# Query, key and value projections in 256-column items, with the attention heads run between their row tiles, in a hybrid decoder step on one core

## What is computed

```
hn = _rmsnorm(x, norm_w)
u = hn @ w_in
z_ssd, xbc, dt_raw, q, k, v, z_att, g_ssd, g_att = jnp.split(u, _split_points(), axis=-1)
...
q = _rope(_rmsnorm(q.reshape(b, t, ATT_HEADS, ATT_HEAD_DIM), q_norm_w), pos)
k = _rope(_rmsnorm(k.reshape(b, t, ATT_HEADS, ATT_HEAD_DIM), k_norm_w), pos)
...
for g, (win, dil) in enumerate(ATT_GROUPS):
    ...
alpha = jax.nn.softmax(jnp.stack(lses, axis=-1), axis=-1)
```

## Time and profile before

| | |
|---|---|
| median of 3 runs | 1186.77 us (1186.63 to 1190.5) |
| profiled execution, its own time | 1187.57 us |
| its span (first to last instruction) | 1185.8 us |
| mean granted TensorE clock | 0.94 of full speed |
| PE busy | 1097.8 us (93%) |
| weight loads busy | 1010.2 us (85%) |
| DVE, ACT, POOL busy | 656.7, 499.4, 219.8 us (55%, 42%, 19%) |
| first row-tile matmul | 18.95 us |
| column stream behind the last head | 426.50 us |

### The profile page before, as it was taken

How to read it: one execution, slowest core, us unless ns; L and a number is a source line. 1 busy time by engine, 2 the same in 40 slices (tenths; PEclk the granted TensorE clock), 3 DMA queues, 4 the chain that set the end, 5 groups by cost and what they waited for, 6 DMA issues and landing times.

```text
span 1185.8 us, 19650 instructions
## 1 busy us (share of the span) xinstructions
PE 1097.8 (93%) x7838; PEld 1010.2 (85%) x7838; DVE 656.7 (55%) x936; ACT 499.4 (42%) x1130; POOL 219.8 (19%) x209
## 2 busy tenths in 40 slices
PE   4999989999999989895999999999998999689998
PEld 3887779977988779775999899898998999689998
DVE  6663527622462347237677677776764466834342
ACT  5334533345333544102554645656445566612210
POOL 0330003400231000000211220221120589500000
PEclk9998899989999899756999999999999999789999
DMA  8546102580242047145056246254446899432221
GB/s 348 213 169 276 55 1 116 213 329 1 107 168 81 1 151 246 58 152 232 1 219 235 109 162 254 110 218 163 182 175 273 343 360 343 155 144 80 100 98 46
DMA packets 29819, 198.14 MB, mean 167 GB/s; under 512 B 4104, under 2 KB 6280, under 8 KB 20224
## 3 DMA queue, kind: packets, MB, share of 16 engines
q1 hardware_dynamic: 25712, 183.35, 40.5%
q0 software_dynamic: 4016, 13.54, 3.0%
HBM read 180.16 MB, written 104.70 MB: 240 GB/s over the span
## 4 chain that ended last, share of the span: by engine, by line
PE 73%; DVE 11%; ACT 7%; issue 4%; DMA 2%; POOL 2%; SPq 0%; DVEq 0%; ACTq 0%; POOLq 0%
PE bank L618 36%; PE bank L590 16%; DVE cacc L1575 2%; PE bank L813 2%; PE bank L715 2%; ACT wH L1136 2%; PE bank L678 2%; PE bank L767 2%; POOL t L1080 2%; PE bank L884 1%; PE bank L654 1%; DVE wL L1511 1%; DMA slot<-in_state_ssm 1%; PE bank L902 1%; PE bank L876 1%
## 5 line engine op out<-in xcount | busy, mean ns | idle before, releaser
L1511 DVE TENSOR_TENSOR wL<-w_raw,wH 128x2048 fp32r<-128x2048 f32 (+1 forms) x63 | 145.0, 2302 | 155.0 <-ACT wH L1136 152.9
L618 PE MATMUL bank<-xH,wH 128*128 128x260 f32 x976 | 207.9, 294 | 8.1 <-DVEq L1455 6.9
L618 PE MATMUL bank<-xH,wL 128*128 128x260 f32 x976 | 198.1, 285 | 0.0
L618 PE MATMUL bank<-xL,wH 128*128 128x260 f32 x976 | 197.8, 284 | 0.0
L1136 ACT CAST wH<-w_raw 128x2048 fp32r<-128x2048 f32 (+1 forms) x63 | 119.2, 1892 | 136.2 <-PE bank L618 84.8
L618 PEld LDWEIGHTS bank<-xH,wH 128*128 128x128 f32 x976 | 152.0, 191 | 18.8 <-issue 16.6
L618 PEld LDWEIGHTS bank<-xH,wL 128*128 128x128 f32 x976 | 152.0, 190 | 0.0
L618 PEld LDWEIGHTS bank<-xL,wH 128*128 128x128 f32 x976 | 152.0, 190 | 0.0
L590 PE MATMUL bank<-wH,xH 128*128 128x512 f32 x336 | 136.7, 407 | 10.0 <-DVE xL L1490 6.0
L590 PE MATMUL bank<-wH,xL 128*128 128x512 f32 x336 | 134.6, 401 | 0.0
L590 PE MATMUL bank<-wL,xH 128*128 128x512 f32 x336 | 134.6, 401 | 0.0
(11 more groups left out here) (285 smaller groups left out, 1916.9 us busy)
## 6 DMA issues: line engine op xcount, KB each, us to landing
w_raw<-in_weights SPq DMA_DIRECT2D x62, 1024.0 KB, 5.3
out_kvs<-in_cache SPq DMA_DIRECT2D x16, 2044.0 KB, 10.2
ring<-in_cache SPq DMA_DIRECT2D x48, 256.0 KB, 3.2
slot<-in_state_ssm SPq DMA_DIRECT2D x16, 512.0 KB, 5.9
out_ssm_s<-slot POOLq DMA_DIRECT2D x16, 512.0 KB, 6.0
out_kvs<-in_cache SPq DMA_DIRECT2D x8, 508.0 KB, 8.8
out_kvp<-st POOLq DMA_DIRECT2D x9, 256.0 KB, 2.3
out_kvp<-vv POOLq DMA_DIRECT2D x9, 256.0 KB, 4.6
```

The costliest lines, as they stand in the source:

```text
L618: mm = pe.matmul(bk[hf].tile[:, 0:HALF], wslot(w, i)[:, k, s * P:(s + 1) * P], x[:, k, hf * HALF:(hf + 1) * HALF], start=(k == 0 and n == ...
L1511: TT(wL[:, i % 2, 0:k * n], raw[:, i % 2, 0:k * n], wH[:, i % 2, 0:k * n].bitcast(F32), ALU.subtract)\
```

## The change

- An item is now (s, x): 256 output columns, which is half a group (x = 0 to 5, four heads), with the **full** contraction of 1024. There are 18 of them, of 1 MB, as before. Their order is q, k, v of half 0, then of half 1, and so on.
- `rows` computes one row tile of an item: 8 k-steps x 3 matmuls of 256 columns, in one of three banks (0 to 2) in turn. `rowtile` and `proj_rows` are gone.
- The steps on a tile are pipelined over slots, a slot being one row tile: `copy` (squares and sums, or the copy of v), a slot later `norm`, then `roped`, then `turn`, with two buffers each of `qn`, `t1`, `t2`. `st` now holds one item; `qT`, `kT` and `vv` are doubled by half group.
- The heads of half group x run beside the rows of half group x + 1, one step (`scores`, `exps`, `probs`, `values`) per slot. Those of the last half group follow behind the last rows, with ("za", 0) between them.
- Banks: rows 0 to 2, scores 3 and 4, transposed probabilities 5, turned rows and previous-chunk probabilities 6, values 7. Some of the later banks are renumbered.
- Stores of k and v rows are one per tile and half group, with semaphores of their own.
- In `ssdE` the second matmul of a pair reads partitions 64 to 127, into which ACT copies the two parts of `ac2` once (in `dtrows`); both banks are taken before the first.

```diff
-    items = [("rm", g, s, half) for g in range(NG) for s in "qkv" for half in range(2)]
+    items = [(s, x) for x in range(HALVES) for s in "qkv"]
...
-BESIDE_HEADS = {1: {0: 7}, 2: {0: 7, 1: 5}}
+SLOT_ROWS = 3 * (NT + 1)
...
+    def side_steps():
+
+        at = {}
+        for n in range(NG * SLOTS):
+            x, m = divmod(n, HH)
+            first, gap = (SLOT_ROWS * (x + 1) + 4 * m, 1) if x < HALVES - 2 else (SLOT_ROWS * (x + 1) + 3 * m, 1)
+            if x == HALVES - 1:
+                first = SLOT_ROWS * HALVES - 2 + 2 * m
+            for d, op in enumerate(("scores", "exps", "probs", "values")):
+                at.setdefault(first + d * gap, []).append((op, n))
+        return at
...
+        mine = at.get(j, [])
+        out.extend(x for x in mine if x[0] == "exps")
+        step("roped", 2)
+        step("norm", 1)
+        step("copy", 0)
+        step("turn", 3)
+        out.extend(x for x in mine if x[0] != "exps")
+
+    for j, (i, t) in enumerate(rows):
+        if t == 0 and ("split", i + 1) not in out:
+            out.append(("split", i + 1))
+        out.append(("rows", i, t))
+        if j == 0:
+            out.append(("rope",))
+        slot(j)
+    j = len(rows)
+    for unit in range(2):
+        za_uses.append(proj("za", 0, unit=unit))
+        _, i, units = out.pop()
+        za_steps += [("proj", i, units, k) for k in range(KD)]
+    late = max(at) + 1 - j
+    for d in range(late):
+        out += za_steps[len(za_steps) * d // late:len(za_steps) * (d + 1) // late]
+        slot(j + d)
...
-        def row_bank(g, s, t):
-
-            return banks[BESIDE_HEADS.get(g, {}).get(t, t) if s == "q" else t]
+        def row_bank(i, t):
+
+            return banks[(i * (NT + 1) + t) % 3]
+
+        def score_bank(n):
+
+            return banks[3 if n < SLOTS else 3 + n % 2]
...
+                elif op == "rows":
+
+                    i, t = a
                     pe.wait_ge(S["weight_low_ready"], i + 1)
...
+                    bk = row_bank(i, t)
+                    bk.take(pe, ("row", i, t))
+                    for kk in range(KD):
+                        if i == t == 0:
+                            pe.wait_ge(S["x_low_ready"], kk + 1)
+                        for n, (x, w) in enumerate(((xH, wH), (xL, wH), (xH, wL))):
+                            mm = pe.matmul(bk.tile[:, 0:HC], x[:, kk, row_columns(i // 6, t)], wslot(w, i)[:, kk, :],
+                                           start=(kk == 0 and n == 0), stop=(kk == KD - 1 and n == 2))
+                    mm.then_inc(bk.filled, 1)
...
+                    pe.wait_ge(S["qk_rows_ready"], qk_count(i, t) + 1)
+                    banks[6].take(pe, ("turn", i, t))
+                    for hp in range(2):
+                        mm = pe.transpose(banks[6].tile[:, hp * P:(hp + 1) * P], st[:, t, hp * P:(hp + 1) * P], ident)
...
                         pe.wait_ge(S["ac_parts_ready"], 1)
+                        pe.wait_ge(S["ac_parts_doubled"], 1)
+                    for e in range(2):
+                        banks[5 + e].take(pe, ("ac", u, e))
                     for e in range(2):
                         bk = banks[5 + e]
-                        bk.take(pe, ("ac", u, e))
-                        pe.matmul(bk.tile[:, :], id2[:, 2 * u + e:2 * u + e + 1].to_broadcast([2 * HEADS, P]), ac2[:, :],
+                        o = 2 * HEADS * e
+                        pe.matmul(bk.tile[:, :], id2[o:o + 2 * HEADS, 2 * u + e:2 * u + e + 1].to_broadcast([2 * HEADS, P]), ac2[o:o + 2 * HEADS, :],
                                   start=True, stop=True, skip_group_check=True).then_inc(bk.filled, 1)
```

More of the change, by code:

```diff
@@ L112, in whole @@
         out.append(proj(*item))
[L114 to L142, removed]
@@ new lines, in plan, with slot, step @@
+    rows = [(i, t) for i in range(3 * HALVES) for t in range(NT + 1)]
+    za_steps = []
+    def slot(j):
+        def step(op, ago):
+            if 0 <= j - ago < len(rows):
+                i, t = rows[j - ago]
+                if op == "copy" or ITEMS[i][0] != "v" and (op != "turn" or t < NT):
+                    out.append((op, i, t))
+        mine = at.get(j, [])
[5 more added lines that the diff above has]
+        out.extend(x for x in mine if x[0] != "exps")
@@ L165, in plan @@
         if i == 3:
-            out.append(("exps",))
+            out.append(("mergeexps",))
         if i == n // 2:
@@ L575, in row_columns @@
                 return slice(0, P) if t == NT else (slice(B + P * t, B + P * (t + 1)) if g == 0 else slice(B + t, R, NT))
-            def proj_rows(i, g, s, half):
-                for t in range(NT + 1):
-                    if s == "q" and t in BESIDE_HEADS.get(g, {}):
-                        continue
-                    bk = row_bank(g, s, t)
-                    if half == 0:
-                        bk.take(pe, ("rm", g, s, t))
-                    cols = row_columns(g, t)
-                    for k in range(4):
-                        kk = 4 * half + k
-                        if t == 0 and (g, s) == (0, "q"):
-                            pe.wait_ge(S["x_low_ready"], kk + 1)
-                        for n, (a, b) in enumerate(((xH, wH), (xL, wH), (xH, wL))):
-                            mm = pe.matmul(bk.tile[:, :], a[:, kk, cols], wslot(b, i)[:, k, :],
-                                           start=(kk == 0 and n == 0), stop=(kk == KD - 1 and n == 2))
-                    if half == 1:
-                        mm.then_inc(bk.filled, 1)
-                    elif t == NT:
-                        mm.then_inc(S["half_item_used"], 1)
-                ends[i] = (banks[NT].filled, banks[NT].uses["rm", g, s, NT]) if half else (S["half_item_used"], i // 2 + 1)
             def proj_cols(i, units, tile, kind, j):
@@ L1792, in _ @@
                     ch.link(V.tensor_copy(ac2[0:HEADS, :], acT[:, :]))
-                    for x in range(2):
+                    for x in range(4):
                         o = x * HEADS
```

469 lines of the change are left out of this document (229 added, 240 removed).

## The result

The changed kernel takes **1342.48 us** in the median of four runs (1338.74 to 1344.7), beside 1186.7 (1186.04 to 1190.5) for the kernel before: ratio 1.1306, 95% interval 1.1282 to 1.133. It is slower, as forecast, but by 156 us and not by 81, and the time lies outside the range of 1235 to 1298. The profiled execution took 1341.62 us, its span is 1339.8.

The account below looks back on a forecast made before the run. PE was taken as the bound, nearly full in row stages and idle in head stages. Its terms summed to 491.3 us against 407.6, +83.7, less 3 for ssdE: +80.7 on 1187.57, so 1268 us, range 1235 to 1298.

Parts of the forecast that it names:

- the strided load: Row tiles of groups 1 and 2: weight loads 16 bytes apart set the pace, 1152 x 0.22 = 253.4 us.
- the sum: PE's work from 18.95 us to the end of the heads, added part by part: 491.3 us against 407.6.
- the SSD pair: ssdE: its two matmuls on different partitions run at once, -3 us taken, within 0 to 3.7 gain less 0.6.
- the forecast of +81: Whole kernel: +80.7 us on the profiled execution's 1187.57, giving 1268 us for the median.
- Row tiles, contiguous: Group-0 and sample tiles: 0.116 us per 256-column matmul, load hidden; 80.7 us and 33.4 us.
- the two measured gaps: Strided loads starting after a PE wait: 0.21 and 0.22 us to the next, the basis for taking 0.22.
- Waits and gaps: Row and head part, PE: 16 us left, made of 2 low clock, 6 piece changes, 4 group-0 heads, 4 tail.
- The part: Row tiles and heads, from 18.95 us to the column stream behind the last head: 491.3 against 407.6, +83.7 us.
- xL at the start: First tile of the first item: wants all eight parts of xL from DVE, done at about 27; 8 us.
- the group-0 heads: Beside the second half's rows: PE waits for ACT's exponentials, up to 1 us for each of four heads, 4 us.
- the chain of a head: Rival: it does not fit its slots, 24 heads cost 2 to 3 us each; 1310 to 1330, chance 0.06.
- the clock falls: Rival, strided part: PE granted 1.2 GHz; sample tiles, transposes and 20 heads double, +100, 1370 us; chance 0.04.

Follow-up runs that it names:

- experiments 1 and 3: Changed kernel with adjacent columns in groups 1 and 2: 1217.2 us; with the earlier kernel's bank list: 1292.45; with that list and adjacent columns: 1167.55 us.
- the experiment: Changed kernel with the earlier bank list and both ssdE matmuls on partitions 0 to 63 again: 1295.62 us.
- experiment 2: Kernel before the change with merge banks 1 and 3 exchanged, so bank 3 is freed last: 1235.45 us, ratio 1.0401.
- experiment 1: Changed kernel with merge banks 2 and 3 freed first: 1334.68 us; with adjacent columns in groups 1 and 2: 1217.2; with both: 1210.47 us.
- experiments 2 and 4: Kernel before with merge banks 1 and 3 exchanged: 1235.45 us; changed kernel with 26 unused matmuls filling PE's wait for bank 3: 1297.15 us.

## Why the prediction was wrong in size

The sign and the mechanism of the strided load held; the sum stopped short of a stage in which I had costed nothing. The experiments give -20 (interleaving with the SSD pair), +125 (stride) and +50 (late bank). That these add up to the measured 156 is no proof by itself, since each was measured against the next. What shows that the two costs are separate is that each has the same size with and without the other: the stride 125.3 and 124.9 us (experiments 1 and 3), the bank 50.0 us with strided columns and 49.7 with adjacent ones. Of the 75 us by which the forecast of +81 fell short, 50 are the bank and 17 the pace of the strided loads. With the bank list of before the time is 1292.45, inside the range but near its upper edge.

- **Row tiles, contiguous.** 0.116 was taken from the column stream; 0.116 was measured within a tile, and 2.86 us for a tile of 24, which is 0.119 each. Right, but for some 3 us over the 41 contiguous tiles.
- **The strided load.** The mechanism was right, and "I take 0.22, nearest to the two measured gaps" was the wrong end of the bounds. The starts are 0.235 apart, which is the upper bound, the pace of strided 512-column matmuls. That pace had been put down to the 512 columns; it fits as well a load that sets it. The two measured gaps were read rightly, but they are those of a first load behind idle time: 0.21 also in the changed kernel, where the loads behind it start 0.235 apart. A strided tile takes 5.64 us instead of 5.28, 17 us in 48 tiles. Of the two rules of the Trainium skill that were weighed, the one of "SBUF — State Buffer", section "Door 1: The DMA port swizzle", held for the step of four columns; the 107 ns of "TensorE: Matmul & The Clock Gate", section "LDWEIGHTS (loading the stationary operand)", fit steps of one and two only.
- **Waits and gaps.** The part gave +106.8 where +83.7 was forecast. 17 of the 23 are the strided loads and 3 the contiguous tiles; the other 3 weren't taken apart. The long waits had the expected sizes: 6.8 us for xL at the start, 4.0 beside the group-0 heads, and no more than 1.3 for anything else. The 4.0 has another cause than the one worked out, though: the wait doesn't end with the exponentials. PE waits ahead of the second group of transposes (L712) for bank 6, which these share with the turned rows, and in the longest of the three waits, 2.30 us, ACT frees it only behind the exponentials, a rounding of weights (1.90 us) and its other copies. So that term was right by luck. PE is idle for 11 us, and the chain of a head fits its slots.
- **The SSD pair.** -3 forecast; -2.9 in the profile, 3.2 by the experiment.
- **The merge banks.** This is the step that failed and took the time out of the range: 50 us for which the sum has nothing. The change lists "Some of the later banks are renumbered", and the sum has no term for it; of the two questions to be asked of each moved thing, who frees it and who takes it next, I asked neither for these banks. The order in which DVE frees them, against the bank that PE wants first, could be read from the code alone. The wait could have been priced as well: DVE's six copies take 0.68 to 1.08 us each in the kernel before, PE's transposes for one of them 0.44, so PE is several microseconds ahead when it has turned the last; experiment 2 gives 4.9 us for it in the kernel before. Its price through the clock, 45 us, no row of the kernel before showed.
- **The clock.** The rival "the clock falls" was put into the strided row tiles, where the clock is 1.00, and argued down with the window of 440 to 480 us. That row shows that this stream keeps the clock it comes with. It doesn't show that the stream earns it: after a wait of 5 us the very same stream, PE busy without a gap, has 0.50 for 90 us. This is 42 us between the first and the last key score, more than the range had on its upper side. The rival's 1370 lies near the measured time by chance: its place, the strided part, kept its clock.
- **The range.** Its lower bound, 1235, doesn't follow from the terms given with it: 12 and 10 below 1268 is 1246. The result doesn't hang on it.

## What to carry over

Loads of a stationary operand whose fp32 words lie 16 bytes apart followed each other here at half the pace of adjacent ones (0.235 us against 0.12), and shorter matmuls uncovered it: before narrowing a matmul, set the pace of its own load, at that step, beside the new pace, and take the slowest pace at which such loads were ever seen to follow each other. When banks or buffers are renumbered, write down for each the order of freeing and the order of taking; a wait of a few microseconds on TensorE has to be priced with the stage behind it, at both levels of the clock. Where such a wait can't be moved, matmuls whose result nobody reads can be cheaper than waiting: here 26 of them gave 45 us back.

## What the runs showed of the chip that was not expected

The granted clock of one and the same stretch has two outcomes. The key stage, with the same instructions and with PE busy without a gap, ran at 1.00 in the kernel before and with the old bank list (47.5 us from the first key score to the last), and at 0.50 in the changed kernel and in the kernel before with two banks exchanged (89.3 us each; the second is shown):

```profile
L767 PE MATMUL bank<-qd,KT x192: 207/352/353, 446.7 to 536.0; 128*128 128x2 f32 x192
```

What went with it were the microseconds ahead of it: an idle time of 5.6 or 4.9 us, and in the two kernels of experiment 1 with the new list two of 0.74 and 0.96 us, were followed by the lower level; a single one of 0.74 to 0.86 us, or 26 matmuls to no purpose in the gap, by the higher. For the long wait experiments 2 and 4 show it to be the cause. For the two short ones it is an inference from the kernels with and without the second. The Trainium skill ("TensorE: Matmul & The Clock Gate", section "Part 1: The HAM clock gate (the "warmup" mystery)") has the throttled level as the default and activity as what releases it. The fall after idleness agrees; that a stream which is busy in every record stays at 1.2 GHz for 90 us does not, so here the measurement decides. Whether the many short matmuls of that stream (two columns, 128 columns) keep it there wasn't tried.
